# A decoder kernel of two blocks: gated delta-net squares turned on TensorE, roots with PSUM copies, and two top-k rounds moved

## What is computed

```python
def gdn_mixer(qkv, z, a_g, b_g, conv_w, a_log, dt_bias, norm_g):
    qkv = jax.nn.silu(causal_depthwise_conv(qkv, conv_w)).astype(jnp.float32)
    q, k, v = jnp.split(qkv, 3, axis=-1)
    q = l2_norm(q.reshape(shp))          # 4 heads of 128: x * rsqrt(sum(x*x) + EPS)
    k = l2_norm(k.reshape(shp))
    ...
    o = gated_delta_rule(q, k, v, g, beta)   # per chunk of 64: (A + I)^-1 by a triangular solve

def dsa_mixer(...):
    ...
        score = jnp.where(causal[None], score, -jnp.inf)
        _, sel = lax.top_k(score, topk)      # topk = 128 of up to 512 keys per query
```

## Time and profile before

| what | us |
|---|---|
| median of 3 runs | 1791.96 (1789.82 to 1793.03) |
| the profiled execution, its own time | 1789.37 |
| its span in the trace | 1787.6 |
| busy in the span: TensorE, GpSimd, VectorE, ScalarE | 1753.5, 1108.3, 936.6, 476.7 |
| TensorE idle, waiting for VectorE's `g_TT` in the inverse | 3.8 in 4 waits |

### The profile page before, as it was taken

How to read it: one execution, slowest core, us unless ns; L and a number is a source line. 1 busy time by engine, 2 the same in 40 slices (tenths; PEclk the granted TensorE clock), 3 DMA queues, 4 the chain that set the end, 5 groups by cost and what they waited for, 6 DMA issues and landing times.

```text
span 1787.6 us, 26170 instructions
## 1 busy us (share of the span) xinstructions
PE 1753.5 (98%) x9182; PEld 1470.2 (82%) x9182; DVE 936.6 (52%) x1537; ACT 476.7 (27%) x963; POOL 1108.3 (62%) x848
## 2 busy tenths in 40 slices
PE   7999999999999999999999999998999999999998
PEld 4888888888988888888888778886878778888887
DVE  4754736465455455554553698797465563213311
ACT  4121221211222223222321226654442422002200
POOL 3657555689754545554447658985155688667862
PEclk9999999999999999999999999999999999999999
DMA  9523222285433223322223332201032333333331
GB/s 352 177 84 95 76 82 76 86 320 166 140 89 86 76 65 94 92 76 74 84 76 95 100 83 59 72 25 36 1 118 59 93 97 101 99 94 94 94 105 49
DMA packets 282164, 176.02 MB, mean 98 GB/s; under 512 B 6064, under 2 KB 272624, under 8 KB 280816
## 3 DMA queue, kind: packets, MB, share of 16 engines
q1 hardware_dynamic: 275024, 151.01, 28.8%
q10 hardware_dynamic: 7072, 24.07, 3.8%
HBM read 172.31 MB, written 2.62 MB: 98 GB/s over the span
## 4 chain that ended last, share of the span: by engine, by line
PE 93%; DVE 4%; SPq 1%; DMA 0%; ACT 0%; issue 0%; ACTq 0%; DVEq 0%
PE acc L400 14%; PE acc L402 14%; PE acc L401 14%; PE ob L400 4%; PE ob L402 4%; PE ob L401 4%; PE acc L430 3%; PE acc L432 3%; PE acc L431 3%; PE sc L1697 2%; PE acc L448 2%; PE acc L449 2%; PE acc L450 2%; PE sc L1602 1%; PE ob L1709 1%; PE acc L1563 1%
## 5 line engine op out<-in xcount | busy, mean ns | idle before, releaser
L800 POOL TENSOR_TENSOR wl<-raw,wh 128x512 fp32r<-128x512 f32 x456 | 639.8, 1424 | 19.3
L797 POOL TENSOR_SCALAR wh<-raw 128x1024 fp32r<-128x1024 f32 (+1 forms) x232 | 273.0, 1177 | 552.0 <-PE acc L402 138.7
L400 PE MATMUL acc<-hh,wh 128*128 128x512 f32 x800 | 324.6, 406 | 1.4 <-ACT sq L1472 1.2
L402 PE MATMUL acc<-hh,wl 128*128 128x512 f32 x800 | 313.1, 391 | 0.0
L401 PE MATMUL acc<-hl,wh 128*128 128x512 f32 x800 | 312.1, 390 | 0.0
L400 PEld LDWEIGHTS acc<-hh,wh 128*128 128x128 f32 x800 | 150.8, 188 | 35.5 <-issue 2.9
L402 PEld LDWEIGHTS acc<-hh,wl 128*128 128x128 f32 x800 | 150.4, 188 | 32.8
L401 PEld LDWEIGHTS acc<-hl,wh 128*128 128x128 f32 x800 | 150.9, 189 | 32.2 <-issue 2.4
L400 PE MATMUL ob<-Yh,wh 128*128 128x512 f32 x256 | 100.5, 393 | 0.0
L402 PE MATMUL ob<-Yh,wl 128*128 128x512 f32 x256 | 99.7, 390 | 0.0
L401 PE MATMUL ob<-Yl,wh 128*128 128x512 f32 x256 | 99.7, 389 | 0.0
(11 more groups left out here) (559 smaller groups left out, 3724.6 us busy)
## 6 DMA issues: line engine op xcount, KB each, us to landing
raw<-in_att_w_in SPq DMA_DIRECT2D x64, 512.0 KB, 3.9
raw<-in_mlp_w SPq DMA_DIRECT2D x64, 512.0 KB, 3.8
raw<-in_ret_w_in SPq DMA_DIRECT2D x48, 512.0 KB, 3.7
ada_w<-in_ada_w ACTq DMA_DIRECT2D x8, 1536.0 KB, 7.4
raw<-in_w_in SPq DMA_DIRECT2D x23, 512.0 KB, 3.6
ada_w<-in_ada_w SPq DMA_DIRECT2D x16, 512.0 KB, 9.1
raw<-in_ret_w_out SPq DMA_DIRECT2D x16, 512.0 KB, 4.2
raw<-in_att_w_out SPq DMA_DIRECT2D x16, 512.0 KB, 4.1
```

What stands on the lines that cost most here:

```text
L400: e.matmul(bank[:, :], wh[:, s, k, :], rhs_high(k), start=(start and k == 0), stop=False)
L402: last = e.matmul(bank[:, :], wl[:, s, k, :], rhs_high(k), start=False, stop=(stop and k == k1 - 1))
L797: e.tensor_scalar(wh[:, s, 0:k1, :], raw[:, s, 0:k1, :], 1.0, 1.0, ALU.mult, ALU.mult).then_inc(high_done, 1)
L800: low = e.tensor_tensor(wl[:, s, k0:k0 + KT // 2, :], raw[:, s, k0:k0 + KT // 2, :], wh[:, s, k0:k0 + KT // 2, :].bitcast(F32), ALU.subtract)
```

## The change

Four edits. (1) `gdn_sums` turns each head's squares on TensorE (four 128 x 128 transposes, output in `sc0`, `sc1` for heads 0 to 4 and `bc` for 5 to 7) and a new VectorE function `gdn_sum` reduces the turned bank along the free axis into a small SBUF table `gss`. Each reuse of a bank waits for the sum that read it, and so do the grams (`sc0`) and the spread of the convolution norm (`bc`). (2) The 56 mixing roots are computed by `roots_bank`, which keeps a copy of each operand in the bank `st`, so that every Newton step has one operand in PSUM. (3) Rounds 10 and 11 stand behind `silu(11)`, ahead of `gQKT`. (4) In the inverse, steps 0 to 3 hold rounds 12 to 15, step 4 the masks 1 and 2, and step 5 mask 3.

```diff
+        def sum_bank(i):
+            return sc[i % 2] if i < 5 else bc
...
             def gdn_sums(i):
                 e.wait_ge(*AC.at(f"g_sq{i}"))
-                c = (0 if TAPPED[i][0] == "q" else 16) + i % GH
-                for t in range(NT):
-                    last = e.matmul(st[:, c + 4 * t:c + 4 * t + 1], gsq[:, i % 2, t * P:(t + 1) * P], ones[:, 0:1],
-                                    start=True, stop=True)
-                last.then_inc(*PE.done(f"g_cols{i}"))
+                e.wait_ge(*V.at({0: "d_sum8", 1: "d_sum9", 5: "g_dld"}.get(i, f"g_ss{i - (2 if i < 5 else 1)}")))
+                turned_squares(e, gsq[:, i % 2, :], sum_bank(i), f"g_cols{i}")
...
+            def gdn_sum(i):
+                c = (0 if TAPPED[i][0] == "q" else 16) + i % GH
+                e.wait_ge(*PE.at(f"g_cols{i}"))
+                e.tensor_reduce(gss[:, c:c + 4 * NT - 3:4], sum_bank(i)[:, :].rearrange("p (t n) -> p t n", t=NT),
+                                AX.X, ALU.add).then_inc(*V.done(f"g_ss{i}"))
...
             keep_round(1)
+            gdn_sum(0)
+            gdn_sum(1)
...
             silu(6)
+            gdn_sum(5)
             keep_round(6)
             gdn_differences(2)
             gdn_differences(3)
             silu(7)
+            gdn_sum(6)
...
             keep_round(8)
+            gdn_sum(7)
             keep_round(9)
...
-            roots(e, 0, 56, "g_roots")
+            for j in (0, 1):
+                x = rs[:, 1, :] if j else w[:, 1, :]
+                e.tensor_scalar(x[:, 0:32], gss[:, :], 0.25, EPS, ALU.mult, ALU.add).then_inc(*V.done())
...
+            roots_bank(e, 0, 56, "g_roots", w)
...
             silu(11)
+            keep_round(10)
+            keep_round(11)
...
-                if n < 6:
-                    keep_round(10 + n)
-                if n == 6:
+                if n < 4:
+                    keep_round(12 + n)
+                if n == 4:
                     keep_mask(1)
                     keep_mask(2)
-                if n == 7:
+                if n == 5:
                     keep_mask(3)
```

More of the change, by code:

```diff
@@ L345, in build @@
         dsc = sb("dsa_q_scale", [P, 16])
+        gss = sb("gdn_square_sums", [P, 32])
         dkc = sb("dsa_k_scale", [P, NT])
@@ L1960, in gdn_grams @@
                     e.wait_ge(*V.at(f"d_sum{8 + t}"))
+                    if t == 0:
+                        e.wait_ge(*V.at("g_ss4"))
                 e.wait_ge(*V.at("g_silu3"))
@@ L2042, in _ @@
                 if p == 21:
+                    e.wait_ge(*V.at("g_ss7"))
                     e.wait_ge(*V.at("g_roots"))
@@ L2921, in _ @@
             keep_round(1)
+            gdn_sum(0)
+            gdn_sum(1)
             keep_round(2)
             silu(3)
+            gdn_sum(2)
             keep_round(3)
@@ L2927, in _ @@
             silu(4)
+            gdn_sum(3)
             gdn_differences(0)
@@ L2931, in _ @@
             silu(5)
+            gdn_sum(4)
             keep_round(5)
             silu(6)
+            gdn_sum(5)
             keep_round(6)
@@ L2943, in _ @@
             e.wait_ge(*PE.at("d_cols2"))
-            e.wait_ge(*PE.at("g_cols7"))
-            e.tensor_scalar(rs[:, 1, 0:32], st[:, 0:32], 0.25, EPS, ALU.mult, ALU.add).then_inc(*V.done())
-            e.tensor_scalar(rs[:, 1, 32:36], st[:, 32:36], 1.0 / (2 * P), EPS, ALU.mult, ALU.add).then_inc(*V.done())
-            step(e, e.tensor_scalar(rs[:, 1, 36:56], st[:, 36:56], 1.0 / DD, EPS, ALU.mult, ALU.add), V)
-            roots(e, 0, 56, "g_roots")
+            e.wait_ge(*V.last())
+            w = root_work(56)
+            for j in (0, 1):
+                x = rs[:, 1, :] if j else w[:, 1, :]
+                e.tensor_scalar(x[:, 0:32], gss[:, :], 0.25, EPS, ALU.mult, ALU.add).then_inc(*V.done())
+                e.tensor_scalar(x[:, 32:36], st[:, 32:36], 1.0 / (2 * P), EPS, ALU.mult, ALU.add).then_inc(*V.done())
+                step(e, e.tensor_scalar(x[:, 36:56], st[:, 36:56], 1.0 / DD, EPS, ALU.mult, ALU.add), V)
+            roots_bank(e, 0, 56, "g_roots", w)
             yk, xk2 = rs[:, 0, 16:32], rs[:, 1, 16:32]
```

## The result

The changed kernel takes 1793.55 us (median of 22 runs) against 1791.86 us, a ratio of 1.0013 with a 95% interval from 1.0007 to 1.0019. In a second comparison it was 1.0008 (0.9999 to 1.0017), which taken alone is not clear of noise. The forecast was 1790.0. The time lies in the range, and within 0.2% of before, but it moved up where I had it down by 2 us. The profiled execution spans 1791.5 us.

A forecast was written before the change was run, and what follows sets the result against it. TensorE bounds the mixing, VectorE the inverse. Squares and shorter roots, against later sums and rounds and uncertain masks, net 2.0 us gained at the score part, carried from 1791.96 to 1790.0; range 1785.5 to 1795.3.

The forecast's parts named there:

- The squares on TensorE: Mixing: 0.35 us per head in place of 0.82, mostly waited away at head 4; TensorE leaves 0.8 us early.
- The sums: Mixing, VectorE: eight reductions of 0.69 us bring waits; round 9 ends at 1158.7, so the roots start 2.5 us late.
- the roots: End of mixing, VectorE: 7.32 us fall to 3.2 through PSUM copies, a gain of 4.1; they end at 1161.9.
- rival D: Roots do not get shorter, so `gQKT` starts at 1187.6; 3.6 to 4.3 us lost, 1795.9; chance 0.12.
- Rounds in front: Ahead of the inverse: two rounds of 5.9 us put the start of `gQKT` at 1183.5, 2.25 us later.
- The price is not paid yet: Start of the inverse: X0 and X1 come about 2 us late, but the pipeline behind has slack.
- The masks: Inverse: masks 1 and 2 take at most 2.4 us undisturbed, 4.7 disturbed; total gain 0.5 to 2.9, 2.0 taken.
- from there nothing on VectorE is long any more: Inverse after `g_TT3`: all rounds done, steps 7 to 10 take 9.3 us without waits, `conv_low` 1.29.
- sign that I had named as refuting the forecast: Forecast wrong if `gQKT` starts outside 1182.5 to 1185, or ScalarE's squares move by more than 1 us.
- rival C: Inverse: TensorE's longer wait brings 3.4 us at 1.2 GHz, costing 1.7 us; 1791.7; chance 0.14.
- Rival B: VectorE nowhere late: masks undisturbed, two column steps behind the roots short; 4.9 us gained, 1787.1; chance 0.24.

The follow-up runs named there:

- e1_squares: Kernel before with only the squares turned and summed by VectorE, roots in the old form, rounds and masks in old places; 1793.70 us, ratio 1.0012.
- e4_squares_roots: Changed kernel with rounds 10 and 11 and the masks put back at their old steps in the inverse; 1789.20 us, ratio 0.9986 to before.
- e9_hold: Changed kernel with GpSimd held before the level matrix of step 6 until VectorE finished masks 1 and 2; 1790.31 us, ratio 1.0001 to before.
- e2_roots: Kernel before with the PSUM copies for the roots alone; 1790.37 us, ratio 0.9996.

## Why the prediction was wrong

**The squares on TensorE.** Right in kind: 0.41 us in place of 0.82, and the gain waited away at head 4 (1.71 us). But 0.3 us was left at the end of the mixing (`c_bc` at 1166.15, before at 1166.44), not 0.8: ScalarE's squares of head 7 came 0.43 us later than before, where I had held them fixed.

**The sums, the roots.** Right: 4.24 us of idling, roots from 1159.20 to 1162.43, forecast 1158.7 to 1161.9. That the gain is 4.1 us and hangs on the copies, `e1_squares` against `e4_squares_roots` bears out: 7.6 us of roots without them, 3.2 with them. My rival D was the wrong picture of that failure: its price is paid first in the mixing, by TensorE's 2.6 us of waits for what follows the roots and the half clock behind them, and `gQKT` is late for that reason.

**Rounds in front.** `gQKT` at 1184.15, forecast 1183.5; the 2.25 us I gave became 2.9. "The price is not paid yet" was wrong. TensorE waits 1.43 and 0.94 us at the first steps (1.5, 1.7 and 0.4 us in the second profile, at full clock) where it waited 0.95 us in all, and `e9_hold`, with short masks, is still 1.5 per mille (2.7 us) above `e4_squares_roots`. Part of that is the late start; how much I can't separate from its long mask 3, its convolution and its lower clock (0.8 us by the slope).

**The masks: the step that failed.** I bounded the pair by 2.4 and 4.7 us and took the middle of what followed, 2.0 us gained, because "both long steps of the pair would have to be long again for the lower end". I treated the lengths as independent luck. They are not: GpSimd runs without a gap at that place, so all three later operations were long, in this execution and in the next of the same program (0.71, 1.25, 1.44, 1.30). And 4.7 was no upper end: 6.8 us occurred. So `g_TT3`, which I had ending at 1203.4 to 1205.7, only began at 1206.14. The second profile, without a half-clock stretch in the inverse, gives the size: a gain of 2.0 asks for `g_TT3` to end near 1204.3, it ended at 1206.7, and the shift, +0.45, is 2.45 above my -2.0. Of these 2.4 us at `g_TT3`, 1.6 are the pair (4.9 us against the 3.3 that my middle implied). Then I wrote "from there nothing on VectorE is long any more", which priced the low parts of the convolution at 1.29 us; they took 1.63, and 2.4 to 2.7 in three of the variants, right on the path to the scores. The eight profiled executions of the changed kernel and its variants with both rounds in front have shifts of +3.2, +0.45, +3.3, +0.5, +3.1, +0.2, +2.9 and +0.6; `e2_roots` and `e4_squares_roots`, in the old order, 0.0 and -0.3. My forecast was -2.0. None of the eight came near it, but they scatter with the half-clock stretches between 1180 and 1274, of which they have 3, 0, 1, 0, 2, 1, 2 and 2, and the kernel before one.

Every sign that I had named as refuting the forecast stayed away: `gQKT` in its window, ScalarE's squares within 1 us, one long wait for `g_TT3`. I had named none for the length of the masks, the term that failed.

**The clock (rival C).** It occurred, more than once, in the profiled execution, and would have passed for the cause. Over many runs the clock was the same before and after, so it does not make the loss against the kernel before; it may well make the gain that squares and roots alone had, and its absence in the changed kernel. The 1.7 us for one stretch was near: 1.3 us per 0.001.

**Rival B** had the right question (are the two-operand steps beside GpSimd long?) and the wrong odds. `e9_hold` is it for the masks, made to happen.

## What to carry to other kernels

Where VectorE is late and GpSimd runs without gaps, a VectorE comparison, scaling or Newton step with its operands in SBUF has no fixed length: mostly its short one or about 1 us more, and in the two worst cases here until GpSimd next paused. The top-k instructions did have one. Look at GpSimd's timeline at the new place before moving such an operation onto a path, and use PSUM operands, fewer operations, or a wait that holds GpSimd. And never read a cause from half-clock stretches in one profile: profile the same program twice, and compare the mean clock over all runs.

## What the hardware showed that I had not expected

- One 128x256 comparison lasted 5.39 us and one scaling of that size 4.47, where 0.53 and 0.3 are their short lengths; both ended with a pause of GpSimd's. The strikes of the top-k rounds, SBUF to SBUF as well, never took over 0.71 us in any profile.
- Holding GpSimd for 1.8 us shortened the masks by 2.8 us and made the changed kernel about 2 us faster, at the edge of the noise, and not slower: GpSimd had slack, VectorE none.
- Executions of one program differ in where TensorE falls to 1.2 GHz: at 1186, 1206 and 1234 in one, at none of them in the next, with the same wait of 2.9 us at step 7.
- Two kernels whose profiles differ by 0.3 us at the end of the stretch (before, and squares and roots) differ by 0.0014 in their times, 2.5 us, and by 0.002 in their mean granted clock.
